# A fourteenth pair of tiles by seven half-size products, and the mLSTM steps of the fourth head set closer

## Chip, cores and metric

One core of one Trainium2 chip runs the whole program. The metric is the device time of one execution in microseconds; less is better. The time before is the median of three runs.

## What is computed

One layer of a hybrid encoder on 1088 columns (1024 of a prompt, 64 of a sample), all in float32: a combined input projection of the normalised x, an mLSTM branch of four heads, a convolution branch, the merge of both, and a feed-forward part. Cut to what matters here:

```python
xn = rmsnorm(x, p['norm_mix_pre'])
proj = xn @ p['w_in']                                  # q, k, v, o, i, f, u (2 x 1024), gates (2 x 1024)
h, C, n, m = mlstm(q, k, v, ig, lf, C, n, m)           # 4 heads, in chunks, a carry C from chunk to chunk
ya = (rmsnorm_heads(h) * jax.nn.sigmoid(o)) @ p['w_proj_a']
glu = u[..., :D_B] * jax.nn.sigmoid(u[..., D_B:])
c, conv_buf = causal_dwconv(glu, conv_buf, p['conv_dw'], p['conv_b'])
c = jax.nn.silu(layernorm(c, p['conv_ln_g'], p['conv_ln_b']))
yb = c @ p['w_proj_b'] + p['b_proj_b']
gt = jax.nn.sigmoid(gates + p['b_merge'])
mix = (gt[..., :D_MODEL] * ya + gt[..., D_MODEL:] * yb) @ p['w_out']
```

## The kernel before

Each float32 product is made of three passes in a rounded format: a weight tile is split into a high part (fhi) and a rest (flo), and so is x (rows 0 to 7 of rx and rows 8 to 15); high by high, high by rest, rest by high. A full output tile is 128 rows by 1088 columns.

The input projection makes its 65 output tiles in two ways. Plain: three slots to a tile (364, 364, 360 columns), each 24 matmuls (`product`, lines 1072 to 1084). By pairs (`pairs`, in `PAIRS_B`): two tiles that belong together (the halves of u, or the two gates of the merge, "g") form a 2 x 2 block matrix with the halves of the columns, and seven half-size products replace eight, each in two column pieces (304 and 240) of 12 matmuls (L1238 to L1240), 14 half products to a pair. The sums of x that this needs overwrite the second halves of the columns in part of rx; the original of them is put aside in DRAM (scr_b12) before the pairs and loaded back at their end. Before there are 13 pairs: six of u and seven of g; the last tile of g is plain.

The order of the stage is written out by hand in tables at the top of the file. `SLOTS` lists the plain slots; slots from S_B (18) on stand behind the pairs: the small "gate" tile (the mLSTM's i and f), then k, v, q of heads 0 to 3, then ga 7 and gb 7, then o 1 to o 7. I count these from the gate on as places 0 to 101, without the six small products `SUM_AFTER` that sum for the layer norm's mean (mu) and variance (var). Tied to places are:

- the 36 steps of the mLSTM (`STEP_AT`; four heads of nine). A step at place s issues its scores in the middle of the product of s (transposes L1146, products L1149), its values behind the product of s+1 (L1166 to L1169), its transposes `rows_out` behind that of s+3 (L1178), its store at s+4. ACT copies what the scores need and takes an exp (L1539 to L1543), DVE multiplies it into wt (L2212, semaphore a_set), DVE adds up hn and updates the carry cb (L2220 to L2251), POOL takes one power, ACT copies the transposed rows to zs (L1566). `rows_out` waits for a_set of all scores issued up to its own place, since both write into one PSUM bank.
- the taps of the depthwise convolution on DVE (`TAPS_AT` in the pairs, 13 a pair; `TAPS_SLOT` in the places, here over 64 of them, two to five a place), 51 operations to each of eight blocks (L2294 and around it).
- the layer norm's passes: `PASS1` (subtract the mean, square) from place 71, `PASS2` (normalise, tanh, multiply, split) at 88 to 99. In `PASS2` ACT does a tanh (L1783) and an Identity (L1786) of 1088 columns in the block's place and a copy (L1791) in the next.

ACT, DVE, SP and POOL walk the same list of slots, each in its own fixed order, and wait on semaphores. In a slot ACT first does the copies and the exp of the scores, then the evacuation (L1600, or L1613 with tanh), at the end of a tile from the ninth on a minus of the next weights (L1499), then zs, hn and its square, then the layer norm's work.

Weights come in a ring of three buffers fraw/flo/fhi (`weights(n)`, L671; from the ninth tile on by POOL). In the pairs the same memory, with four more slots, is a ring of ten for the half weights: slot `aslot(i, prod)` = (7i + POS[prod] + 6) mod 10. `ring_free(n)` gives the half product after which ring buffer n of the plain weights is free of the last pair's. SP's order in the last pair is:

```python
                    else:
                        sp.wait_ge(grp_done, ring_free(N_A))
                        weights(N_A)
                        sp.wait_ge(grp_done, b_at(i, 5, 1))
                        sp.dma_start(rx[:, 0:4, HALF:T].bitcast(F32), scr_b12[0]).then_inc(const_in, 16)
                        sp.dma_start(rx[:, KB:KB + 4, HALF:T].bitcast(F32), scr_b12[1]).then_inc(const_in, 16)
                        sp.wait_ge(grp_done, ring_free(N_A + 1))
                        weights(N_A + 1)
```

N_A is 5, the gate tile. TensorE runs the pairs and then waits for these loads (`pe.wait_ge(const_in, 96)`) and for the last pieces' evacuation before the gate's first product (L1284). The order of the 14 half products is (1,0) (1,1) (5,0) (5,1) (6,0) (6,1) (2,0) (7,0) (7,1) (2,1) (4,0) (4,1) (3,0) (3,1).

Of the kernel before, what the change touches and what calls it, by code (L numbers as in the profile page):

```python
# [12 lines left out]
KB = D // P  # L13
# [42 lines left out]
def in_tiles():  # L56

    def pair(k):
        return [("ua", k), ("ub", k)]

    def head(h, kinds):
        return [(kind, 2 * h + b) for kind in kinds for b in range(2)]

    def one(kind, a, b):
        return [(kind, m) for m in range(a, b)]

    return (pair(0) + pair(1) + one("o", 0, 1)
            + [("gate", 0)] + head(0, "kvq") + head(1, "kvq") + head(2, "kvq") + head(3, "kvq")
            + [("ga", 7), ("gb", 7)] + one("o", 1, KB))


IN_TILES = in_tiles()
# [6 lines left out]
N_A = 5  # L79
S_B = 3 * XN + 3 * (N_A - 3)  # L80
PAIRS_B = [("u", 2), ("g", 0), ("g", 1), ("u", 3), ("g", 2), ("u", 4), ("g", 3), ("u", 5), ("g", 4), ("u", 6), ("g", 5),
           ("u", 7), ("g", 6)]
NB = len(PAIRS_B)
OPS = 7 * NB
POS = {1: 0, 5: 1, 6: 2, 2: 3, 7: 4, 4: 5, 3: 6}
# [18 lines left out]
def done(s):  # L104

    return s + 1 + (14 * NB if s >= S_B else 0)
# [12 lines left out]
def hi_of(n):  # L119
# [1 line left out]
    return n + 1 + (OPS if n >= N_A else 0)  # L121


SUM_AFTER = {S_B + 66: ("mu", 0), S_B + 67: ("mu", 1), S_B + 70: ("mu", 2),
             S_B + 83: ("var", 0), S_B + 86: ("var", 1), S_B + 87: ("var", 2)}


def in_slots():

    slots = []  # L130
    for r, at in enumerate(WSLOTS):
        slots.append(at)
        if r in SUM_AFTER:
            name, c = SUM_AFTER[r]
            slots.append(((name, 0), c))
# [31 lines left out]
STEPS = [(h, j) for h in range(NH) for j in range(NSTEP)]  # L167
FULL = [s for s, (t, c) in enumerate(SLOTS) if t[0] not in ("mu", "var")]
NTH_FULL = {s: r for r, s in enumerate(FULL)}
STEP_AT = [S_B + 22 + 2 * i for i in range(len(STEPS))]  # L170
STEP_IN = {at: i for i, at in enumerate(STEP_AT)}
STEPS_END = FULL[STEP_AT[-1] + 3]

# [8 lines left out]
def rows_before(i):  # L182

    return sum(at + 3 < STEP_AT[i] for at in STEP_AT)


def scores_before(i):

    return sum(at <= STEP_AT[i] + 3 for at in STEP_AT)

# [4 lines left out]

TAPS_AT = [6] + [12 + 13 * i for i in range(NB)]
TAPS_SLOT = [TAPS_AT[NB]]
for r_ in range(64):
    left_ = NOP * KB - TAPS_SLOT[-1]
    TAPS_SLOT.append(TAPS_SLOT[-1] + (2 if r_ < 10 else 5 if r_ < 22 else left_ // (64 - r_)))  # L200
N_BY_DVE = 8
BY_POOL = [sum(1 for i in range(N_BY_DVE, N_IN) if i % 3 == s) for s in range(3)]
C_STORED = 32 * KB // 2
# [27 lines left out]
STORE_SLOT = {k: S_B + r + 1 for r in range(len(TAPS_SLOT) - 1) for k in convs_by(TAPS_SLOT[r], TAPS_SLOT[r + 1])}  # L231


PASS1 = {FULL[S_B + 71 + 3 * k // 2]: k for k in range(KB)}
PASS2 = {FULL[S_B + at]: k for k, at in enumerate((88, 89, 91, 92, 94, 96, 97, 99))}
C_HI = (0, 2, 4, 12, 14, 6, 8, 10)
TANH_OUT = [t for t in IN_TILES if t[0] in ("ga", "gb", "o")]

# [90 lines left out]
def build(nc, x, wts, wdn, par, gate_par, c_in, conv_halo, ffn_halo, y_out, c_out, m_out,  # L329
# [200 lines left out]
    with ExitStack() as ctx:  # L530
# [137 lines left out]
        def _(sp):  # L668
# [101 lines left out]
            for s, ((kind, k), c) in enumerate(SLOTS):  # L770
# [79 lines left out]
                if s == SLOT["mu", 0, 0]:  # L850
# [4 lines left out]
                    for j in range(2):  # L855
                        sp.dma_start(cs[j][:, :], scr_c[j]).then_inc(cs_in[j], 16)
                j = PASS1.get(s - 1)
                if j is not None:
                    sp.wait_ge(xc_set, j + 1)
                    sp.dma_start(scr_xc[j], cs[j % 2][:, :]).then_inc(c_sto[j % 2], 16)  # L860
                    if j + 2 < KB:
                        sp.wait_ge(csq_sq, j + 1)
                        sp.wait_ge(c_sto[j % 2], C_STORED + 16 * (j // 2 + 1))
                        sp.dma_start(cs[j % 2][:, :], scr_c[j + 2]).then_inc(cs_in[j % 2], 16)
                if s == min(PASS2) - 2:
                    for j in range(2):
                        sp.wait_ge(c_sto[j], C_STORED + 16 * KB // 2)
                for j in range(KB):
                    if s == (min(PASS2) - 2 if j < 2 else min(PASS2) + 2 if j < 5 else STEPS_END):
                        sp.wait_ge(grp_done, done(s - 1))  # L870
                        sp.dma_start(fz[:, C_HI[j] + 1, :], scr_xc[j]).then_inc(blk_in[j], 16)
                if s == FULL[STEP_AT[-1] + 4] + 1:
                    for j in range(2):
# [616 lines left out]
        def _(act):  # L1490
# [54 lines left out]
            def values(i):  # L1545
                h, j = STEPS[i]
                p = i % 2
                if j:
                    act.wait_ge(nq_full, i + 1)
                    if i >= 2:  # L1550
                        act.wait_ge(zt_set, i - 1)
                    act.activation(hn[p][:, :], bank(5, 0, VW), ACT.Copy, scale=gt[:, 16 * j + 4 + h:16 * j + 5 + h])\
                        .then_inc(t1_set, 1)
                act.wait_ge(hn_set, i + 1)
                if i >= 2:
                    act.wait_ge(z_full, i - 1)
                act.activation(zt[p][:, :], hn[p][:, 0:DH], ACT.Square, accum_out=sm[p][:, 3:4]).then_inc(ssq, 1)
# [148 lines left out]
            for s, ((kind, k), c) in enumerate(SLOTS):  # L1706
# [64 lines left out]
                if i is not None:  # L1771
                    values(i)
                j = PASS1.get(s)
                if j is not None:
# [3 lines left out]
                    act.activation(csqt[:, :], cs[j % 2][:, :], ACT.Square).then_inc(csq_sq, 1)  # L1778
                j = PASS2.get(s)
                if j is not None:  # L1780
# [6 lines left out]
                                   scale=halfs[:, at:at + 1]).then_inc(nth, 1)  # L1787
                j = PASS2.get(s - 1)
                if j is not None:
# [302 lines left out]
        def _(dve):  # L2092
# [338 lines left out]
            for s, ((kind, k), c) in enumerate(SLOTS):  # L2431
# [36 lines left out]
                for todo in taps_at(s):  # L2468
                    taps(*todo)
                    if todo[2] == NOP:  # L2470
                        add_sum(todo[0])
                j = PASS1.get(s)
                if j is not None:
# [4 lines left out]
                    if j:  # L2478
                        add_square(j - 1)
                if s - 1 == max(PASS1):  # L2480
                    add_square(KB - 1)
                j = PASS2.get(s - 2)
                if j is not None:
                    dve.wait_ge(c_hi, j + 1)
                    dve.tensor_tensor(rz[:, C_HI[j] + 1, :], fz[:, C_HI[j] + 1, :], rz[:, C_HI[j], :].bitcast(F32),
                                      ALU.subtract).then_inc(c_lo, 1)
                j = PASS2.get(s)
                if j is not None:
# [424 lines left out]
```

## Time and profile before

| what | us |
|---|---|
| median of three runs | 1926.76 (1926.02 to 1927.43) |
| the profiled execution | 1926.55 |
| its span, first to last instruction | 1924.6 |
| TensorE (PE) busy | 1904.2, 99% |
| VectorE (DVE) busy | 1297.1, 67% |
| ScalarE (ACT) busy | 834.7, 43% |
| GpSimd (POOL) busy | 69.6, 4% |
| mean of what the DMA moved | 125 GB/s |

The profile is of one execution; times in it are counted from its first instruction. "Busy" is the union of an engine's instructions; a matmul's record is longer than its distance to the next, because matmuls overlap, so costs on TensorE are read from the distance of starts or from windows. L-numbers are lines of the kernel. A wait is put down to the semaphore that came last.

### The profile page before, as it was taken

What the parts mean: (1) busy time and instruction counts of PE and PEld (TensorE: products, weight loads), DVE (VectorE), ACT (ScalarE), POOL (GpSimd) and SP (SyncE); (2) the same over time, 40 slices, a digit from 0 to 9 for tenths busy, and PEclk for the clock granted to TensorE, in tenths of its full rate; (3) what the DMA queues carried; (4) which work ended last, traced back from release to release, by engine and by line L of the source; (5) the groups of instructions that cost most, each with busy time, mean ns of one, the idle gap of its engine ahead of it and who ended that gap; (6) DMA issues with size and microseconds to landing.
All of it is one profiled execution on the core that took longest, in us unless ns stands there. A gap on an engine that the chain in (4) does not pass through costs nothing.

```text
span 1924.6 us, 32360 instructions
## 1 busy us (share of the span) xinstructions
PE 1904.2 (99%) x13095; PEld 1880.2 (98%) x13095; DVE 1297.1 (67%) x1991; ACT 834.7 (43%) x1534; POOL 69.6 (4%) x122
## 2 busy tenths in 40 slices
PE   9999999999999999999999999999999999999997
PEld 8999999999999999999999999999999999999997
DVE  7798889697777725364444468977777676646363
ACT  5454444422333334573122345654455444645342
POOL 0000000011111111110000000000000000000000
PEclk9999999999999999999999999999999999999999
DMA  3323232454343348668131323221222122556654
GB/s 133 125 84 128 96 108 86 160 121 101 86 117 89 94 115 232 183 185 335 61 137 44 129 73 107 90 80 68 83 75 80 68 90 97 194 191 217 206 173 154
DMA packets 108675, 240.24 MB, mean 125 GB/s; under 512 B 19052, under 2 KB 58732, under 8 KB 108528
## 3 DMA queue, kind: packets, MB, share of 16 engines
q1 hardware_dynamic: 99600, 205.66, 31.5%
q0 software_dynamic: 8928, 32.51, 7.6%
q8 instruction: 105, 1.72, 0.4%
q14 instruction: 42, 0.34, 0.1%
HBM read 182.20 MB, written 55.94 MB: 124 GB/s over the span
## 4 chain that ended last, share of the span: by engine, by line
PE 90%; DVE 5%; ACT 2%; issue 1%; DMA 1%; SPq 0%; POOL 0%; DVEq 0%; ACTq 0%; POOLq 0%
PE ps L1079 12%; PE ps L1080 12%; PE ps L1081 12%; PE ps L1438 7%; PE ps L1436 7%; PE ps L1437 7%; PE ps L1238 4%; PE ps L1239 4%; PE ps L1240 4%; PE ps L1454 4%; PE ps L1455 4%; PE ps L1456 4%; PE ps L1169 1%; PE ps L1166 1%; PE ps L1149 1%
## 5 line engine op out<-in xcount | busy, mean ns | idle before, releaser
L1079 PE MATMUL ps<-rx,fhi 128*128 128x364 f32 (+2 forms) x1120 | 375.1, 335 | 1.2 <-DMA flo<-wts 1.1
L1080 PE MATMUL ps<-rx,fhi 128*128 128x364 f32 (+2 forms) x1120 | 364.4, 325 | 0.0
L1081 PE MATMUL ps<-rx,flo 128*128 128x364 f32 (+2 forms) x1120 | 364.2, 325 | 0.0
L1079 PEld LDWEIGHTS ps<-rx,fhi 128*128 128x128 f32 x1120 | 210.7, 188 | 4.0 <-issue 1.6
L1080 PEld LDWEIGHTS ps<-rx,fhi 128*128 128x128 f32 x1120 | 210.7, 188 | 1.3
L1081 PEld LDWEIGHTS ps<-rx,flo 128*128 128x128 f32 x1120 | 210.5, 188 | 0.0
L1454 PE MATMUL ps<-ghi,dhi 128*128 128x384 f32 (+1 forms) x528 | 173.2, 328 | 3.0 <-DVE glo L2733 2.2
L1455 PE MATMUL ps<-glo,dhi 128*128 128x384 f32 (+1 forms) x528 | 172.3, 326 | 0.0
L1456 PE MATMUL ps<-ghi,dlo 128*128 128x384 f32 (+1 forms) x528 | 172.3, 326 | 0.0
L2726 DVE TENSOR_TENSOR dlo<-draw,dhi 128x1408 fp32r<-128x1408 f32 x48 | 77.7, 1625 | 119.0 <-ACT dhi L1985 119.0
L1238 PE MATMUL ps<-rx,ahi 128*128 128x240 f32 (+1 forms) x416 | 120.3, 289 | 0.6 <-DVE v L2390 0.5
L1985 ACT ACTIVATE dhi<-draw 128x1408 fp32r<-128x1408 f32 x48 | 66.1, 1381 | 125.4 <-DMA draw<-wdn 125.3
L1239 PE MATMUL ps<-rx,ahi 128*128 128x240 f32 (+1 forms) x416 | 120.0, 288 | 0.0
L1240 PE MATMUL ps<-rx,alo 128*128 128x240 f32 (+1 forms) x416 | 119.8, 288 | 0.0
L1600 ACT ACTIVATE qkv<-ps 128x364 f32<-128x364 f32 (+1 forms) x72 | 34.1, 474 | 172.8 <-PE ps L1081 172.8
L1454 PEld LDWEIGHTS ps<-ghi,dhi 128*128 128x128 f32 x528 | 99.1, 188 | 4.6 <-DVE glo L2733 2.9
L1455 PEld LDWEIGHTS ps<-glo,dhi 128*128 128x128 f32 x528 | 99.1, 188 | 0.3
L1456 PEld LDWEIGHTS ps<-ghi,dlo 128*128 128x128 f32 x528 | 99.1, 188 | 0.0
L1878 ACT ACTIVATE ub<-ps 128x304 f32<-128x304 f32 (+1 forms) x132 | 50.9, 402 | 103.3 <-PE ps L1438 97.8
L2294 DVE SCALAR_TENSOR_TENSOR f_e<-f_s,hsum,f_e 128x559 f32<-128x559 f32 x120 | 95.6, 796 | 0.0
L2294 DVE SCALAR_TENSOR_TENSOR f_a<-glub,pars,f_a 128x559 f32<-128x559 f32 x120 | 95.5, 796 | 0.0
L1438 PE MATMUL ps<-rz,ulo 128*128 128x304 f32 (+1 forms) x320 | 92.8, 290 | 0.0
(345 smaller groups left out, 5329.9 us busy)
## 6 DMA issues: line engine op xcount, KB each, us to landing
draw<-wdn SPq DMA_DIRECT2D x48, 704.0 KB, 4.2
uraw<-wts SPq DMA_DIRECT2D x44, 512.0 KB, 4.4
fhi<-wts POOLq DMA_DIRECT2D x31, 512.0 KB, 7.2
flo<-wts POOLq DMA_DIRECT2D x31, 512.0 KB, 6.3
fraw<-wts SPq DMA_DIRECT2D x27, 512.0 KB, 3.8
araw<-wts SPq DMA_DIRECT2D x52, 256.0 KB, 2.8
scr_g<-cva SPq DMA_DIRECT2D x22, 512.0 KB, 2.6
graw<-scr_g SPq DMA_DIRECT2D x43, 192.0 KB, 4.0
```

Source lines behind the costliest of these rows:

```text
L1079: pe.matmul(b, hi[:, w], src[:, his[k], cols], start=(k == 0), stop=False)
L1080: pe.matmul(b, hi[:, w], src[:, los[k], cols], start=False, stop=False)
L1081: mm = pe.matmul(b, lo[:, w], src[:, his[k], cols], start=False, stop=(k == KB - 1))
L1238: pe.matmul(b, ahi[s][:, c], bhi[:, k, :], start=(fresh and k == 0), stop=False, skip_group_check=True)
L1239: pe.matmul(b, ahi[s][:, c], blo[:, k, :], start=False, stop=False, skip_group_check=True)
L1240: mm = pe.matmul(b, alo[s][:, c], bhi[:, k, :], start=False, stop=(k == 3), skip_group_check=True)
L1436: pe.matmul(b, whi[:, c], bhi[:, k, :], start=(fresh and k == 0), stop=False, skip_group_check=True)
L1438: mm = pe.matmul(b, wlo[:, c], bhi[:, k, :], start=False, stop=(k == 3), skip_group_check=True)
L1454: pe.matmul(b, dhi[n % 2][:, kk], ghi[g % N_G][:, 0:w], start=(k == 0), stop=False, skip_group_check=True)
L1455: pe.matmul(b, dhi[n % 2][:, kk], glo[g % N_G][:, 0:w], start=False, stop=False, skip_group_check=True)
L1456: mm = pe.matmul(b, dlo[n % 2][:, kk], ghi[g % N_G][:, 0:w], start=False, stop=(k == FB - 1), skip_group_check=True)
L2294: dve.scalar_tensor_tensor(acc[:, :], src[:, i:i + w], tapw, acc[:, :], ALU.mult, ALU.add).then_inc(tap, 1)
```

## The change

The fourteenth pair ("g", 7) joins the list, and the plain tiles ga 7 and gb 7 leave it, with their six slots. Everything that depends on the number of pairs or slots follows by the tables: the rings' turns, the taps (13 more in the pairs), the counts of semaphores. The places are now 0 to 95. The fourth head's nine steps stand at 75, 76, 77, 79, 80, 81, 83, 84 and 86; heads 1 and 2 begin at 39 and 57 with a distance of two as before. mu and var move eight and six or seven places up, both passes of the layer norm seven and six. The taps left for the places are spread over 56 of them instead of 64.

```diff
@@ in_tiles
             + [("gate", 0)] + head(0, "kvq") + head(1, "kvq") + head(2, "kvq") + head(3, "kvq")
-            + [("ga", 7), ("gb", 7)] + one("o", 1, KB))
+            + one("o", 1, KB))
@@
 PAIRS_B = [("u", 2), ("g", 0), ("g", 1), ("u", 3), ("g", 2), ("u", 4), ("g", 3), ("u", 5), ("g", 4), ("u", 6), ("g", 5),
-           ("u", 7), ("g", 6)]
+           ("u", 7), ("g", 6), ("g", 7)]
@@
-SUM_AFTER = {S_B + 66: ("mu", 0), S_B + 67: ("mu", 1), S_B + 70: ("mu", 2),
-             S_B + 83: ("var", 0), S_B + 86: ("var", 1), S_B + 87: ("var", 2)}
+SUM_AFTER = {S_B + 58: ("mu", 0), S_B + 59: ("mu", 1), S_B + 62: ("mu", 2),
+             S_B + 77: ("var", 0), S_B + 79: ("var", 1), S_B + 80: ("var", 2)}
@@
-STEP_AT = [S_B + 22 + 2 * i for i in range(len(STEPS))]
+STEP_AT = [S_B + (22, 39, 57, 75)[h] + (2 * j if h < 3 else 11 * j // 8) for h, j in STEPS]
@@
-for r_ in range(64):
+for r_ in range(56):
     left_ = NOP * KB - TAPS_SLOT[-1]
-    TAPS_SLOT.append(TAPS_SLOT[-1] + (2 if r_ < 10 else 5 if r_ < 22 else left_ // (64 - r_)))
+    TAPS_SLOT.append(TAPS_SLOT[-1] + (2 if r_ < 10 else 5 if r_ < 22 else left_ // (56 - r_)))
@@
-PASS1 = {FULL[S_B + 71 + 3 * k // 2]: k for k in range(KB)}
-PASS2 = {FULL[S_B + at]: k for k, at in enumerate((88, 89, 91, 92, 94, 96, 97, 99))}
+PASS1 = {FULL[S_B + 64 + 3 * k // 2]: k for k in range(KB)}
+PASS2 = {FULL[S_B + at]: k for k, at in enumerate((82, 83, 85, 86, 88, 90, 91, 93))}
```

## Rows read from the trace of the kernel before

**Rows 1.** The page: busy time by engine, and the chain by engine.
```profile
PE 1904.2 (99%) x13095; PEld 1880.2 (98%) x13095; DVE 1297.1 (67%) x1991; ACT 834.7 (43%) x1534; POOL 69.6 (4%) x122
...
PE 90%; DVE 5%; ACT 2%; issue 1%; DMA 1%; SPq 0%; POOL 0%; DVEq 0%; ACTq 0%; POOLq 0%
```

**Rows 2.** Window: us, busy of PE, PEld, DVE, ACT, POOL; clock; DMA share, GB/s.
```profile
355.40:879.20 523.80, 522.74 (x3152) 509.43 (x3152) 346.55 (x706) 223.75 (x480) 67.02 (x104) 1.00 0.50 134
```

**Rows 3.** TensorE's waits, 355 to 880 us: total us, times, longest.
```profile
PE ps L1079 <- DMA flo<-wts: 1.1, 1, 1.1
```

**Rows 4.** Windows of one line's matmuls: ten pairs (L1240), twelve slots (L1081).
```profile
122.92:334.26 211.34, 161.50 (x560) 105.82 (x561) 1.00 0.31 106
...
367.37:415.28 47.91, 31.54 (x96) 18.03 (x96) 1.00 0.42 106
```

**Rows 5.** Timeline of SP's issues in the last pair: start us, us, what.
```profile
340.31 0.33 SPq L671 DMA_DIRECT2D fraw<-wts  x1
340.69 0.59 SPq L751 DMA_DIRECT2D rx<-scr_b  x1
...
349.35 0.35 SPq L671 DMA_DIRECT2D fraw<-wts  x1
```

**Rows 6.** Timeline of TensorE where the pairs end.
```profile
355.22 0.33 PE L1284 MATMUL ps<-rx,fhi 128*128 128x364 f32 x1
```

**Rows 7.** Windows of the last pair; DMA share and GB/s stand last.
```profile
341.50:343.20 1.70, 1.70 (x17) 1.70 (x16) 1.65 (x3) 0.42 (x1) 0.00 (x0) 1.00 0.79 269
343.20:349.60 6.40, 6.40 (x53) 6.40 (x53) 1.50 (x4) 2.12 (x4) 0.00 (x0) 1.00 0.91 346
349.60:350.60 1.00, 1.00 (x10) 1.00 (x9) 1.00 (x3) 0.00 (x0) 0.00 (x0) 1.00 0.38 111
```

**Rows 8.** DMA issues from 320 to 375 us: KB each, median us to landing.
```profile
fraw<-wts SPq DMA_DIRECT2D x3, 512.0 KB, 3.8
```

**Rows 9.** Timeline of DVE: two taps, then the step and its wait.
```profile
625.46 0.80 DVE L2294 SCALAR_TENSOR_TENSOR f_a<-glub,pars,f_a 128x559 f32<-128x559 f32 x1
626.17 0.80 DVE L2294 SCALAR_TENSOR_TENSOR f_d<-glub,pars,f_d 128x560 f32<-128x560 f32 x1
...
629.16 0.43 DVE L2220 TENSOR_TENSOR hn<-ps,hn 128x257 f32<-128x257 f32 x1 [1.48 <-ACT hn L1552]
```

**Rows 10.** The chain that ended last, two successive steps of the first head.
```profile
459.44 0.87 PE ps L1166 x4
470.70 0.87 PE ps L1166 x4
```

**Rows 11.** Timeline of TensorE: rows_out behind a slot, scores in the next.
```profile
796.85 0.38 PE L1178 MATMUL ps<-ident,zt 128*128 128x128 f32 x2
...
801.23 0.60 PE L1146 MATMUL ps<-ident,qkv 128*128 128x128 f32 x4
```

**Rows 12.** Timeline of ACT in the fourth head, beside the layer norm's second pass.
```profile
822.63 0.45 ACT L1613 ACTIVATE spl<-ps 128x360 f32<-128x360 f32 x1
822.98 1.05 ACT L1499 ACTIVATE flo<-fhi 128x1024 fp32r<-128x1024 f32 x1
823.93 0.61 ACT L1566 ACTIVATE zs<-ps,mnq 128x128 f32<-128x128 f32 x2
824.43 0.48 ACT L1552 ACTIVATE hn<-ps,gt 128x257 f32<-128x257 f32 x1
...
825.82 1.28 ACT L1783 ACTIVATE fz<-fz,halfs 128x1088 f32<-128x1088 f32 x1
827.13 1.30 ACT L1786 ACTIVATE fz<-fz,halfs 128x1088 f32<-128x1088 f32 x1
828.34 1.10 ACT L1791 ACTIVATE rz<-fz 128x1088 fp32r<-128x1088 f32 x1
829.34 0.36 ACT L1539 ACTIVATE vt<-ps 128x256 f32<-128x256 f32 x1
```

**Rows 13.** Timeline of DVE: the product of the scores that follow these.
```profile
830.29 0.29 DVE L2212 TENSOR_TENSOR wt<-ps,wt 128x128 f32<-128x128 f32 x1 [2.52 <-ACT wt L1543]
```

## The prediction

> **What bounds the kernel now.** I read the page first: TensorE is busy 1904.2 of 1924.6 us and holds 90% of the chain that ended last [rows 1]. So a change pays only by taking matmuls away or by a wait of TensorE that it ends, and costs what it makes TensorE wait. Next the windows by stage: from the first gate product at 355.4 us to the end of the input projection at 879.2 TensorE is busy 522.7 of 523.8 us at a granted clock of 1.00 [rows 2], and the list of waits has a single one in that stretch, 1.1 us for the last weight tile [rows 3]. There is no idle time to win in the stage that the change reorders. The question is what the new order makes late.
>
> **The matmuls, removed and added.** The two last gate tiles leave the list of slots, six slots of 24 matmuls; a fourteenth pair of 14 half products of 12 matmuls comes in. Ten pairs (560 matmuls of one line, 56 a pair) took 211.34 us, 21.13 each; twelve plain slots without a step (96 of one line, 8 a slot) took 47.91 us, 3.99 each [rows 4]. Removed 6 x 3.99 = 23.95 us, added 21.13: TensorE gets 2.8 us back. The 36 mLSTM steps, the six sums for mu and var and everything behind the stage are the same work. The evacuations (tanh of six slots against ACT and DVE pieces, sums and splits of the half weights) lie beside TensorE in both forms: thirteen pairs run at the matmuls' own pace already, so the fourteenth costs its matmuls.
>
> **The restored half of x: a queue that is moved.** During the pairs half of the columns of rx holds sums; the original was put aside in scr_b12 and SP loads it back (2 x 1088 KB) during the last pair, because the gate tile behind the pairs needs it (PE's wait for const_in 96). SP does that behind `wait ring_free(N_A)`, then weights(5), then the two loads. ring_free(5) is the last use of ring slots 0 and 1 of the ten slots for half weights. They turn with the number of pairs, slot = (7i + POS + 6) mod 10. For i = 12 slots 0 and 1 are products 1 and 5, the first four of the last pair's 14. For i = 13 they are products 2 and 7: the wait moves to the tenth of 14. In the trace of before SP issued weights(5) at 340.31 and the reloads from 340.69, and weights(6), whose wait was for the same tenth product, at 349.35 [rows 5]. The gate's first matmul followed the pairs at 355.22, without a gap [rows 6]. So SP will issue the reload with only 6.0 us of products left, instead of 15.
>
> How long it takes: behind the issue of the weights the DMA moved 269 GB/s to 343.2 (the weights), 346 GB/s to 349.6 (6.4 us x 346 = 2.2 MB, the reload) and fell to 111 GB/s in the last microsecond [rows 7]. From 340.31 that is 9.3 us to the fall, 10.3 to the end of that window. After the change both transfers stand in the same queue in the same order. From 349.35 the reload lands at 358.7 to 359.7 of the old clock, and TensorE, ready at 355.4, **waits 3.3 to 4.3 us; I take 3.8**. Before, the same landing lay 4.8 us ahead of its use, which is why no row shows a wait. Bounds: 2.75 MB at the 346 GB/s of the best window with nothing around it are 7.9 us, 6.0 of them covered, so 1.9 us; and 4.5, if the last packets and their signal take as long as they can in these windows. Behind the waiting gate matmuls stands all of TensorE; nothing catches up, because it is the bound.
>
> Other things hang on the same wait. ACT takes weights(5) in its order ahead of the last two product-4 pieces: it lands some 3.8 us after its issue [rows 8], at 353.1, its copy of 1024 columns takes about 1 us, the pieces reach to 355: just in time, nothing more than the reload. weights(6) now waits for the last product, lands behind the reload at about 361, and is wanted when the gate's 8 us are over (367): covered by the gate tile; if the reload were early, its slack would still be 2 us. weights(7) follows it. All other moves of SP, the neighbours' nb, c_out and cb transfers, have two or more slots of slack; 0.
>
> **The taps.** With 13 more taps in the pairs, 227 are left for 56 slots; the last eleven get five each, where before no slot with steps had more than four. In a two-slot period with eight taps DVE waits 1.48 us for ACT's hn, and a tap follows the last at 0.71 us [rows 9]: two more take 1.42. It fits by a hair; a lag recovers and TensorE's use of DVE's results is a slot later. 0, up to 1.
>
> **The steps closer together.** A step with two slots takes 11.25 us (459.44 to 470.70 [rows 10]); less 2 x 3.99 that is 3.27 on TensorE. 2.38 of it are rows_out and values (796.85 to 801.23 less half a product of 2.0 [rows 11]), 0.87 the scores. Heads 1 and 2 start one place earlier and keep the spacing of two: 0. The fourth head stands at 75, 76, 77, 79, 80, 81, 83, 84, 86. Before, scores and rows_out never fell in one slot. Now they do at 79, 80, 83, 84, 86, and rows_out waits for a_set of the scores begun half a product, 2.0 us, earlier, since both use one bank. Normally a_set is there 1.1 us ahead of it. At 79 and 80 nothing else is large on ACT: 0. From 82 on the layer norm's second pass is there too. I follow ACT from the end of place 82's product (0): TensorE does rows_out and values to 2.4, place 83 ends at 7.3, its rows_out at 7.5, scores of 84 at 9.5 to 10.3, product end 12.3, where rows_out wants a_set. ACT from 7.3, by the distance of successive starts [rows 12]: evacuation 0.35, minus 0.95, two zs 0.5 (823.93 to 824.43), then tanh 1.3, Identity 1.2 and the copy of the block before 1.0: 12.6. Only then the new scores' vt, kw and exp up to DVE's product, 0.95 (829.34 to 830.29), and the product itself, 0.3 [rows 12, 13]: 13.9. TensorE **waits 1.6 us** at place 84. Place 83 has 0.5 us left by the same count, place 86 0.5. Bounds: 0 (ACT half a block ahead) and 3 (83 and 86 lose theirs too). Layer norm's first pass keeps its pattern, seven places earlier; the six sums move with it; from place 87 on (eight before the last) everything stands as before, the 1.1 us for the last weights included.
>
> **Sum.** -2.8 + 3.8 + 1.6 = +2.6 us. The profiled execution took 1926.55 us (span 1924.6 and 1.95 around it), 0.2 under the median of the three runs, 1926.76. So 1926.55 + 2.6 = 1929.2, 1929.3 against the median. A measurement of this kernel can tell 0.2%, 3.9 us, from no change: this is +0.13%, within it.
>
> **The clock at the gap.** The granted clock is 1.00 across every stretch read and the longest wait in the stage is 1.1 us [rows 2, 3]; a gap of 3.8 us has no like in the trace. The Trainium skill (TensorE: Matmul & The Clock Gate, Part 1) says that an idle stretch takes the array to 1.2 GHz, and activity back to 2.4: this speaks against the change, and no row here shows it. By rows, the gate tile is 8 us of matmuls at 2.4 GHz (355.4 to 363.4); at 1.2 it would take up to 8 more, at least 0. By that rule the sum would be between +2.6 and +10.6.
>
> **The rivals.**
> - *The reload hides after all and the steps don't bite:* the time is 1926.8 - 2.8 = 1924.0. For it: nothing waited there before. Against: the transfer's 7.9 us are more than the 6.0 left. 6 in 100. To be over 0.2% faster something unseen must go too, as the last weights' 1.1 us.
> - *The clock falls at the gap (slower):* place, the gate tile; price 0 to 8 us, middle 4; it decides from a drop that lasts 1.3 us of TensorE's work. 1929.3 + 4 = 1933.3. For: the gap is near three times any wait of the stage. Against: it is short, and the matmuls around it are dense. 12 in 100.
> - *ACT becomes the bound in the fourth head (slower):* its backlog of 5.3 us a slot against a slot of 4.86 repeats at 83, 84 and 86 with evacuations late as well: 3 waits of 1.6 to 2 in place of one, +3.5: 1932.8. For: ACT is the only engine near full there. Against: places 84 and 85 bring no new block beyond one. 14 in 100.
> - *The reload stalls and the steps are free:* 1927.7, inside the forecast's range.
>
> **The numbers.** Forecast 0.62 (with the last rival in it; own range 1925.9 to 1931.5: -2.8 + 1.9 + 0 to -2.8 + 4.5 + 3), hidden 0.06, clock 0.12, ACT 0.14, others 0.06. The range reaches from the hidden case's 1924.0 to 1933.5, which leaves out the clock's upper half and tails. Slower by over 0.2% (above 1930.6): the two slower rivals, 0.24, and a sixth of the forecast's range; 0.34 rounded to 0.32 for their mild halves. Faster 0.05, same 0.63.
>
> **What would show it.** Right: in SP's order the loads of rx come after 349.35 + 21.1 = 370.5; TensorE's list of waits has a new row at the gate's line, L1284, of 3.3 to 4.3 us put down to the DMA rx<-scr_b or const_in; a wait of 1 to 3 us at rows_out's line L1178 on DVE's wt in the fourth head, and no other new row over 1 us; the stage from the gate to the end of the projection is 22.4 us shorter (23.95 less 1.6). Wrong: no gate wait (the loads were faster), a granted clock under 1 behind it, waits of TensorE on ACT's evacuations, or DVE late for mu.

## The result, and the profile after

The changed kernel takes **1930.1 us**, the median of nine runs (1929.19 to 1933.14); the kernel before, on the same chip, 1926.38 (1924.92 to 1927.43). The recorded ratio is 1.0023, 95% interval 1.0014 to 1.0032. The change is slower: by 3.7 us between the medians, just inside the 0.2% (3.9 us) that the prediction called no change, and by 0.23% (4.4 us) by the ratio, just outside it. The interval lies on both sides of that mark. Forecast were 1929.3 and +2.6. The profiled execution took 1929.81 us.

The page of the changed kernel: its span, busy time by engine, and TensorE's busy tenths.

```profile
span 1928.0 us, 32466 instructions
PE 1902.0 (99%) x13119; PEld 1878.2 (97%) x13119; DVE 1305.4 (68%) x2008; ACT 839.3 (44%) x1543; POOL 66.9 (3%) x118
...
PE   9999999899999999999999999999999999999997
```

TensorE is busy 2.2 us less than in [rows 1], and the span is 3.4 us longer. The one 8 among TensorE's tenths is the slice from 337 to 386 us: the gap is there. Next the waits of TensorE in the changed kernel from 370 to 885 us, the stretch in which [rows 3] had one row:

```profile
PE ps L1284 <- DMA rx<-scr_b: 5.3, 1, 5.3
PE ps L1178 <- issue: 1.5, 1, 1.5
PE ps L1079 <- DMA flo<-wts: 1.0, 1, 1.0
```

Both new rows are at the lines that the prediction named. The second was foretold at 1.6. The first is 5.3 where 3.8 was foretold. Here is TensorE's own timeline where the pairs end (start, duration, what, idle before it); [rows 6] answers to it:

```profile
375.43 0.28 PE L1240 MATMUL ps<-rx,alo 128*128 128x240 f32 x1
380.96 0.67 PE L1284 MATMUL ps<-rx,fhi 128*128 128x364 f32 x1 [5.26 <-DMA rx<-scr_b]
381.43 0.51 PE L1285 MATMUL ps<-rx,fhi 128*128 128x364 f32 x1
...
384.43 0.33 PE L1285 MATMUL ps<-rx,fhi 128*128 128x364 f32 x1
...
390.58 0.32 PE L1079 MATMUL ps<-rx,fhi 128*128 128x364 f32 x1
```

Behind the gap a matmul takes 0.51 us, and from 384.43 on 0.33. The windows of the same stretch name the reason; the granted clock stands ahead of the DMA's share and its GB/s:

```profile
375.80:381.00 5.20, 0.04 (x1) 0.04 (x1) 0.34 (x1) 1.59 (x2) 2.10 (x6) 1.00 1.02 391
381.00:382.40 1.40, 1.40 (x5) 1.40 (x6) 0.00 (x0) 0.00 (x0) 0.00 (x0) 0.50 0.98 398
382.40:384.00 1.60, 1.60 (x7) 1.60 (x6) 0.48 (x1) 1.06 (x1) 0.00 (x0) 0.50 0.46 188
...
385.44:388.10 2.66, 2.66 (x18) 2.66 (x18) 2.66 (x5) 2.06 (x4) 0.00 (x0) 1.00 0.00 0
```

From 381.0 to 384.0 the engine had 1.2 of its 2.4 GHz, after 5.3 us without a matmul; it got the rest back while it worked. From the last matmul of the pairs to the first of the tile behind the gate (L1079) it is 390.58 - 375.43 = 15.15 us. In the kernel before the same two matmuls stand at

```profile
355.10 0.28 PE L1240 MATMUL ps<-rx,alo 128*128 128x240 f32 x1
...
363.19 0.33 PE L1079 MATMUL ps<-rx,fhi 128*128 128x364 f32 x1
```

8.09 us apart. The loss is 7.06 us. TensorE starts the gate tile 5.4 us later behind the pairs, which is the wait, and the tile takes 9.62 us (380.96 to 390.58) where it took 7.97 (355.22 to 363.19): 1.65 us of half clock. I call this distance **D**; it serves in all experiments below.

The issues of SP in the changed kernel, to be held against [rows 5]:

```profile
369.71 0.33 SPq L671 DMA_DIRECT2D fraw<-wts  x1
370.09 0.59 SPq L751 DMA_DIRECT2D rx<-scr_b  x1
370.72 0.63 SPq L752 DMA_DIRECT2D rx<-scr_b  x1
375.73 0.83 SPq L671 DMA_DIRECT2D fraw<-wts  x2
```

The reload is issued with 5.6 us of products left. And the place in the fourth head: ACT's timeline in the changed kernel, from the evacuation at the end of place 83's product to that of place 84, and TensorE's first instruction behind its wait ([rows 12] show the same operations before):

```profile
823.72 0.47 ACT L1613 ACTIVATE spl<-ps 128x360 f32<-128x360 f32 x1 [0.91 <-PE ps L1081]
824.09 1.05 ACT L1499 ACTIVATE flo<-fhi 128x1024 fp32r<-128x1024 f32 x1
825.04 0.62 ACT L1566 ACTIVATE zs<-ps,mnq 128x128 f32<-128x128 f32 x2
825.53 1.30 ACT L1783 ACTIVATE fz<-fz,halfs 128x1088 f32<-128x1088 f32 x1
826.87 1.30 ACT L1786 ACTIVATE fz<-fz,halfs 128x1088 f32<-128x1088 f32 x1
828.07 1.09 ACT L1791 ACTIVATE rz<-fz 128x1088 fp32r<-128x1088 f32 x1
829.07 0.36 ACT L1539 ACTIVATE vt<-ps 128x256 f32<-128x256 f32 x1
...
829.69 0.30 ACT L1543 ACTIVATE wt<-wt 128x128 f32<-128x128 f32 x1
```

```profile
830.03 0.29 DVE L2212 TENSOR_TENSOR wt<-ps,wt 128x128 f32<-128x128 f32 x1 [4.23 <-ACT wt L1543]
```

```profile
830.42 0.41 PE L1178 MATMUL ps<-ident,zt 128*128 128x128 f32 x2 [1.54 <-issue]
```

The three long operations of the layer norm's second pass stand between the evacuation and the scores' copies, in the order in which the prediction laid them out; from 823.72 to vt at 829.07 it is 5.35 us, and the prediction counted 5.3 (7.3 to 12.6). The profile puts TensorE's wait down to "issue", that is, to nothing that it shows. The kernel has rows_out wait for DVE's product of the scores (L2212), and that product, held up for ACT's exp until 830.03, ends at 830.3, 0.1 us before TensorE starts.

**The sum.** The window from the end of the pairs to the end of the input projection, in the changed kernel ([rows 2] is the same stretch before):

```profile
375.72:884.12 508.40, 500.60 (x3009) 487.07 (x3010) 338.00 (x694) 219.81 (x473) 64.35 (x100) 1.00 0.50 136
```

It is 15.4 us shorter (523.8 before): 23.95 less 7.06 and 1.5 is 15.4. With the 21.13 us of the fourteenth pair that makes +5.7. The spans differ by 3.4, so 2.3 lie outside the stage. The first matmul of the pairs starts at 78.28 us, before at 79.08; in the other runs below this start falls anywhere from 77.95 (e10) to 79.72 (e1), whatever the kernel, so these 0.8 are scatter. The rest, 1.5, lies behind the stage, where TensorE's waits show 1.1 of it: at L1454 2.2 us for glo and 0.8 for dlo before, 1.5 and 0.6 after, at L1436 0.8 before and 0.6 after. From the first matmul behind the projection (879.05 before, 883.94 after) to the end of the span it is 1045.6 us before, 1045.2 and 1045.1 in the two other kernels with 13 pairs (e2, e5), 1044.1 in the changed kernel and 1044.2 to 1045.0 in the eight others with 14 pairs. By the means of the two kinds some 0.9 us of the 1.5 come with the new order in every such kernel, and the rest is scatter. Why the waits are shorter is open.

### The profile page after: what moved, and what is told of

Its sections match the earlier page's. It is cut to its first block, busy times and chain, and to the rows that moved or that the text cites. A ratio compares the mean times of both kernels' runs of the same rounds, so it can differ in the third digit from the quotient of the medians.

```text
span 1928.0 us, 32466 instructions
## 1 busy us (share of the span) xinstructions
PE 1902.0 (99%) x13119; PEld 1878.2 (97%) x13119; DVE 1305.4 (68%) x2008; ACT 839.3 (44%) x1543; POOL 66.9 (3%) x118
## 4 chain that ended last, share of the span: by engine, by line
PE 92%; DVE 4%; DMA 2%; ACT 1%; issue 1%; SPq 0%; POOL 0%; DVEq 0%; ACTq 0%; POOLq 0%
PE ps L1079 12%; PE ps L1081 12%; PE ps L1080 12%; PE ps L1438 7%; PE ps L1436 7%; PE ps L1437 7%; PE ps L1238 5%; PE ps L1239 5%; PE ps L1240 5%; PE ps L1454 4%; PE ps L1455 4%; PE ps L1456 4%; PE ps L1169 2%; PE ps L1166 1%; PE ps L1149 1%
## 5 line engine op out<-in xcount | busy, mean ns | idle before, releaser
L1079 PE MATMUL ps<-rx,fhi 128*128 128x364 f32 (+2 forms) x1072 | 359.4, 335 | 1.1 <-DMA flo<-wts 1.0
L1080 PE MATMUL ps<-rx,fhi 128*128 128x364 f32 (+2 forms) x1072 | 348.6, 325 | 0.0
L1081 PE MATMUL ps<-rx,flo 128*128 128x364 f32 (+2 forms) x1072 | 348.5, 325 | 0.0
L1079 PEld LDWEIGHTS ps<-rx,fhi 128*128 128x128 f32 x1072 | 201.7, 188 | 3.7 <-issue 1.5
L1080 PEld LDWEIGHTS ps<-rx,fhi 128*128 128x128 f32 x1072 | 201.7, 188 | 1.3
L1081 PEld LDWEIGHTS ps<-rx,flo 128*128 128x128 f32 x1072 | 201.5, 188 | 0.0
L1454 PE MATMUL ps<-ghi,dhi 128*128 128x384 f32 (+1 forms) x528 | 173.2, 328 | 2.1 <-DVE glo L2733 1.5
L1238 PE MATMUL ps<-rx,ahi 128*128 128x304 f32 x448 | 129.6, 289 | 0.6 <-DVE v L2390 0.5
L1239 PE MATMUL ps<-rx,ahi 128*128 128x304 f32 x448 | 129.2, 288 | 0.0
L1240 PE MATMUL ps<-rx,alo 128*128 128x304 f32 x448 | 129.0, 288 | 0.0
L1454 PEld LDWEIGHTS ps<-ghi,dhi 128*128 128x128 f32 x528 | 99.1, 188 | 3.6 <-DVE glo L2733 2.2
```

What stands on the lines that cost most here:

```text
L1079: pe.matmul(b, hi[:, w], src[:, his[k], cols], start=(k == 0), stop=False)
L1080: pe.matmul(b, hi[:, w], src[:, los[k], cols], start=False, stop=False)
L1081: mm = pe.matmul(b, lo[:, w], src[:, his[k], cols], start=False, stop=(k == KB - 1))
L1238: pe.matmul(b, ahi[s][:, c], bhi[:, k, :], start=(fresh and k == 0), stop=False, skip_group_check=True)
L1239: pe.matmul(b, ahi[s][:, c], blo[:, k, :], start=False, stop=False, skip_group_check=True)
L1240: mm = pe.matmul(b, alo[s][:, c], bhi[:, k, :], start=False, stop=(k == 3), skip_group_check=True)
```

## The experiments

All ten (e1 to e10) were timed in five rounds beside the kernel before, whose median was 1926.24 us beside e1 to e4, 1925.84 beside e5 to e8, 1926.25 beside e9 and 1926.35 beside e10. The theory at the start: the change is worth -2.8 us of matmuls, the reload behind the late wait costs 7 (a wait and the half clock behind it), and the steps 1.5. The rivals: the loss at the gate is the clock's and not the load's; the load is slow because other transfers share its way; the steps cost nothing or much more.

**e1. The reload first.** On the changed kernel, SP issues the reload ahead of the wait for the ring, and the gate's weights behind it:

```diff
-                        sp.wait_ge(grp_done, ring_free(N_A))
-                        weights(N_A)
                         sp.wait_ge(grp_done, b_at(i, 5, 1))
                         sp.dma_start(rx[:, 0:4, HALF:T].bitcast(F32), scr_b12[0]).then_inc(const_in, 16)
                         sp.dma_start(rx[:, KB:KB + 4, HALF:T].bitcast(F32), scr_b12[1]).then_inc(const_in, 16)
+                        sp.wait_ge(grp_done, ring_free(N_A))
+                        weights(N_A)
```

> The changed kernel with SP's order in the last pair turned: the two reloads of rx right behind product (5,1), weights(5) behind them with its own wait. Theory (the loss is the late reload): the wait of 5.3 us at L1284 is gone, and with it the 3.4 us at half clock that followed it (1.7 us), so 7.0 us less than the changed kernel: about 1923.1, and 3 us under the kernel before; the 1.5 us at L1178 stays. Rival (the gate tile is late for another reason, its weights or the pieces of product 4, which weights(5) still delays): a wait of 2 us or more stays at L1284 and the gain over the changed kernel is under 4 us.

Measured: 1924.44 us (1924.16 to 1926.23, 11 runs), ratio to before 0.9992 (0.9983 to 1.0001), 5.7 us under the changed kernel. Of its waits of TensorE from 350 to 885 us the one at the gate, and ACT at the gate's evacuation:

```profile
...
PE ps L1284 <- ACT g L1594: 1.4, 1, 1.4
...
```

```profile
380.78 1.06 ACT L1494 ACTIVATE fhi<-fraw 128x1024 fp32r<-128x1024 f32 x1 [2.03 <-DMA fraw<-wts]
...
383.38 0.47 ACT L1594 ACTIVATE g<-ps 4x364 f32<-4x364 f32 x1
```

The wait for rx is gone and the half clock with it; D is 386.67 - 376.86 = 9.81. A new wait took 1.4 of the gain: ACT stands for 2.0 us in the copy of the next weights, which its order puts ahead of the gate's evacuation, and TensorE's third gate product, for a bank of PSUM, waits until ACT has emptied it (L1594, done at 383.85; TensorE goes on at 383.89). In the changed kernel the late reload had hidden that. So the late reload is the cause of the loss at the gate, and the next wait in the queue was 1.4 us long.

**e2. The late reload alone, in the kernel before.** Nothing of the change but the moment of the wait: the tenth product of the last of 13 pairs.

```diff
-                        sp.wait_ge(grp_done, ring_free(N_A))
+                        sp.wait_ge(grp_done, b_at(i, 2, 1))
```

> The kernel before (13 pairs), with weights(5) and the reload held back until the tenth half product of the last pair, as the ring makes it in the changed one. Theory: a wait of 4 to 5.5 us on the DMA rx<-scr_b at L1284 appears here too, without any fourteenth pair, perhaps with some us at half clock behind it: 4 to 7 us slower than before, about 1930.4 to 1933.4. Rival (the wait belongs to the fourteenth pair's own traffic): under 2 us slower.

Measured: 1932.36 us (1930.57 to 1934.56, 5 runs), ratio 1.0035 (1.0022 to 1.0047), +6.1. The window of the gap with the first matmuls behind it, and TensorE's first matmul after it:

```profile
356.40:363.20 6.80, 3.81 (x13) 3.81 (x14) 1.41 (x2) 1.06 (x1) 0.13 (x2) 0.50 0.98 363
```

```profile
359.39 0.67 PE L1284 MATMUL ps<-rx,fhi 128*128 128x364 f32 x1 [5.09 <-DMA rx<-scr_b]
```

A wait of 5.1 us, half clock behind it for 3.8 us, D = 369.15 - 354.02 = 15.13: the changed kernel's loss at the gate, from one moved wait, without a fourteenth pair and without closer steps.

**e3 and e6. The gap filled with matmuls.** To part the clock from the wait: small matmuls of a constant into a bank not in use stand ahead of TensorE's wait for rx, first 46, then 23.

```diff
                     pairs()
+                    pe.wait_ge(c11_set, 2 * NB)
+                    for _ in range(46):
+                        pe.matmul(bank(7, 0, P), ones[:, :], ident[:, :], start=True, stop=True)
                     pe.wait_ge(const_in, 96)
```

> The changed kernel with 46 small matmuls (ones by ident into an idle PSUM bank, result unused, some 4.9 us) between the last half product and the wait for the reload; nothing is left out. Theory (the idle engine loses its clock, and the first gate matmuls pay 1.7 us): the granted clock stays at 1.00 through the gate tile, its first product takes 2.7 us instead of 4.5, and the time is 1.7 us under the changed kernel's, about 1928.4; the reload lands when it did. Rival (the clock falls for another reason, or its fall costs nothing): no difference, 1930.1 within 0.5.

Measured: 1933.76 us (1933.35 to 1935.32, 5 runs), ratio 1.0042 (1.0029 to 1.0054). The groups of TensorE from 375 to 387 us:

```profile
L1249 PE MATMUL ps<-ident,ones 128*128 128x128 f32 x92 | 10.4, 275 | 0.0
```

46 instructions stand there as 92, from 375.29 to the gate's first matmul at 385.48: 10.2 us, where I had counted on about 5. The filling was twice too long and ended 4.5 us behind the moment at which TensorE began in the changed kernel (380.96). The clock stayed at 1.00 in every window, as expected, but the time says nothing. So again with half as many:

> The test of the busy gap again, with 23 small matmuls instead of 46: each of them runs as two passes of 0.107 us, so 46 filled 9.8 us and ended 4.9 us behind the landing; 23 fill 4.9 of the 5.3. Theory: the clock stays at 1.00, the first gate product ends 1.7 us earlier than in the changed kernel, time 1928.4. Rival (the fall of the clock costs nothing): 1930.1 within 0.5.

Measured: 1930.34 us (1928.35 to 1931.06, 11 runs), ratio 1.0021 (1.0012 to 1.003). Two windows, in the filling and behind it, and two of the waits:

```profile
376.00:381.50 5.50, 5.50 (x52) 5.50 (x51) 1.06 (x3) 2.44 (x3) 2.14 (x6) 1.00 1.05 362
383.00:385.00 2.00, 2.00 (x14) 2.00 (x13) 0.00 (x0) 0.58 (x1) 0.00 (x0) 1.00 0.53 217
```

```profile
PE ps L1079 <- DMA flo<-wts: 1.4, 1, 1.4
PE ps L1287 <- DMA rx<-scr_b: 0.6, 1, 0.6
```

No half clock, and D = 390.77 - 376.66 = 14.11, 1.04 less than in the changed kernel although the gate tile began 6.03 us behind the last matmul of the pairs (382.69), where it was 5.53. The tile itself took 8.08 us in place of 9.62. But TensorE then waited 0.4 us longer for the last weights, and the medians do not differ (1930.34 and 1930.1). What the profiles show is that the half clock follows the idle time and that without it the gate tile is 1.5 us shorter; what it is worth in the whole time I could not resolve. It is the smaller part in any case: the load is the cause.

**e4. The next weights held back.** Does the reload take long because weights(6) and (7), issued at 375.73, share its way? On the changed kernel:

```diff
                         sp.wait_ge(grp_done, ring_free(N_A + 1))
+                        sp.wait_ge(const_in, 96)
                         weights(N_A + 1)
```

> The changed kernel with SP holding weights(6) and weights(7) back until the reload has landed. Theory (these two, issued at 375.7 while the reload was under way, share the DMA engines with its last third and made the wait 5.3 instead of the 3.8 forecast): the wait at L1284 falls to 3.8 to 4.6 us, and k 0's first product then waits for its weights only if they take over 7 us. Time 1 us under the changed kernel, or less if the half clock falls otherwise. Rival (the reload is slow by itself): the wait stays at 5.0 to 5.5 us.

Measured: 1930.28 us (1929.4 to 1931.44, 11 runs), ratio 1.0023 (1.0014 to 1.0032), no gain. The wait at the gate is 4.7 instead of 5.3. Whether these 0.6 are the price of sharing is not settled. From the issue of weights(5) to TensorE's start it is 11.25 us in the changed kernel and 10.69 here, but 11.75 in e6 (370.94 to 382.69), which makes the same transfers as the changed kernel: one profile each, and a scatter of 0.5. The windows of the reload (issued from 370.17 on) and the first gate matmul:

```profile
369.80:378.30 8.50, 5.99 (x48) 5.79 (x46) 1.88 (x4) 3.94 (x5) 2.14 (x6) 1.00 0.88 309
...
378.80:380.50 1.70, 0.01 (x1) 0.01 (x1) 0.00 (x0) 0.00 (x0) 0.00 (x0) 1.00 0.10 37
```

```profile
380.49 0.43 PE L1285 MATMUL ps<-rx,fhi 128*128 128x364 f32 x1 [4.71 <-DMA rx<-scr_b]
```

The DMA's rate in 40 equal steps of 0.35 us from 368 to 382 us:

```profile
GB/s 0 0 0 0 0 0 0 70 140 187 246 339 406 301 323 342 336 361 385 404 392 395 348 373 367 385 404 410 429 317 87 50 50 50 12 0 0 0 94 70
```

This is the larger part of the overshoot. With nothing beside it the transfer is all but over at 378.8, and TensorE starts 1.7 us later. In that time the queues move 37 GB/s, at a tenth of the sixteen engines' time: a few last packets until about 380.2 (10.4 us behind the issue of the weights), and TensorE goes on at 380.49. The fall of the rate is not the landing.

The shorter wait brought nothing: D is 390.62 - 375.51 = 15.11, as in the changed kernel. The half clock came here too, from 381.07 on, 0.6 us after TensorE had begun again, and the third product of the gate waited 0.2 for ACT, whose copy of the held-back weights was now late.

**e5. The closer steps alone, in the kernel before.** The fourth head at 81, 82, 83, 85, 86, 87, 89, 90 and 92 (six behind the changed kernel's), with 13 pairs and the layer norm where it was.

```diff
-STEP_AT = [S_B + 22 + 2 * i for i in range(len(STEPS))]
+STEP_AT = [S_B + (22 + 2 * i if h < 3 else 81 + 11 * j // 8) for i, (h, j) in enumerate(STEPS)]
```

> The kernel before (13 pairs, 102 places) with the fourth head alone set at 81, 82, 83, 85, 86, 87, 89, 90, 92, where the changed kernel has it relative to the layer norm's second pass. Theory (scores and rows_out in one slot wait for ACT's backlog): one wait of 1.5 us at L1178, near place 90, and 1 to 2 us slower than before, about 1927.7; no wait at L1284 and no half clock. Rival (closer steps cost nothing, the wait at L1178 belongs to the shortened stage): the time of before within 0.5.

Measured: 1932.22 us (1931.7 to 1933.11, 5 runs), ratio 1.0032 (1.0019 to 1.0045), +6.4. Waits of TensorE, ACT ahead of the longest, and the window behind it:

```profile
PE ps L1146 <- ACT kw L1540: 4.4, 2, 3.0
PE ps L1178 <- issue: 1.5, 2, 0.9
```

```profile
770.63 1.11 ACT L1778 ACTIVATE csqt<-cs 128x1088 f32<-128x1088 f32 x1 [4.77 <-DVE csq L2327]
771.64 0.37 ACT L1539 ACTIVATE vt<-ps 128x256 f32<-128x256 f32 x1
```

```profile
773.00:776.00 3.00, 3.00 (x21) 3.00 (x22) 0.17 (x1) 0.00 (x0) 0.00 (x0) 1.00 1.00 366
```

L1178 costs the 1.5 that it costs in the changed kernel, in two parts. The other 4.4 are of a kind that I had not thought of: in this arrangement the last blocks of the first pass fall among the closer steps, ACT waits 4.8 us in its order for DVE's square (L2327), and the scores' copies wait behind it. The clock stayed at 1.00 behind this gap of 3.0 us. That the change's earlier layer norm avoids these late copies is how I read it, for e5 also keeps the taps and the six sums where they were, and no run moved the first pass alone. This run shows the 1.5 at L1178 again; it does not price the steps alone.

**e7. The evacuation of the gate freed.** On e1: ACT's copy of weights(6) moves from the end of the pairs to behind the gate's first evacuation, DVE's rest of it likewise.

```diff
@@ ACT, end of the pairs
-                whole(N_A + 1)
@@ ACT, each slot
                 evac(s, kind, k, c)
+                if s == S_B:
+                    whole(N_A + 1)
@@ DVE, end of the pairs
-                rest(N_A + 1)
@@ DVE, each slot, behind the taps
+                if s == S_B:
+                    rest(N_A + 1)
```

> The kernel with the reload first, and ACT's copy and DVE's rest of the k 0 weights (weights(6), which now land 4 us behind the pairs) moved from ahead of the gate's first evacuation to behind it. Theory (the 1.4 us at L1284 on ACT's g come from ACT sitting in that copy's wait while the gate's first piece is ready): that wait goes, 1.4 us under the reload-first kernel, about 1923.0. Rival (the copy is then late for k 0): a wait on flo of as much at L1079.

Measured: **1923.38 us** (1922.44 to 1924.45, 11 runs), ratio 0.9986 (0.9978 to 0.9995).

```profile
PE ps L1178 <- issue: 1.5, 1, 1.5
PE ps L1079 <- DMA flo<-wts: 0.7, 1, 0.7
```

D is 384.66 - 376.40 = 8.26, within 0.2 of the kernel before. Both losses at the gate are gone, and what the fourteenth pair promises by its matmuls is there: from the first matmul of the pairs to the last of the projection it is 798.4 us (79.27 to 877.66), 799.8 before (79.08 to 878.88), 1.4 less for the -2.8 of matmuls and 1.5 of the steps. The whole time fits only with the part behind the stage that I cannot explain: 1925.84 (before, in this series) - 2.8 + 1.5 - 1.5 is 1923.0.

**e8. The second pass later.** On e7, to take the backlog out of ACT's way at place 84, the second block of the second pass goes from 83 to 84.

```diff
-PASS2 = {FULL[S_B + at]: k for k, at in enumerate((82, 83, 85, 86, 88, 90, 91, 93))}
+PASS2 = {FULL[S_B + at]: k for k, at in enumerate((82, 84, 85, 86, 88, 90, 91, 93))}
```

> The same with the layer norm's second block in place 84 instead of 83, so that ACT comes to the scores of place 84 without that block's tanh and Identity (2.5 us) ahead of them. Theory: the wait of 1.5 us at L1178 goes; at most 0.5 comes back at place 86, where the copy of that block now stands ahead of the scores: 1.0 to 1.5 us less again, about 1921.8. Rival (the backlog only moves): a wait of 1 us or more at place 86, or at the last weights, and no gain.

Measured: 1924.52 us (1923.71 to 1926.07, 11 runs), ratio 0.9994 (0.9985 to 1.0003), 1.1 us more than e7. TensorE's timeline at place 86, and the window behind it:

```profile
837.83 0.66 PE L1178 MATMUL ps<-ident,zt 128*128 128x128 f32 x2 [2.36 <-issue]
```

```profile
837.80:841.00 3.20, 3.17 (x11) 3.20 (x12) 3.20 (x3) 2.26 (x4) 1.46 (x2) 0.50 0.67 223
```

The rival was right: the wait moved two places on and grew, and now it, too, is followed by half clock.

**e9 and e10. The steps themselves further apart.** On e7, the fourth head's eighth block goes from place 84 to 85, then (e10, with 12 in place of the 11 below) its ninth from 86 to 87 as well.

```diff
-STEP_AT = [S_B + (22, 39, 57, 75)[h] + (2 * j if h < 3 else 11 * j // 8) for h, j in STEPS]
+STEP_AT = [S_B + (22, 39, 57, 75)[h] + (2 * j if h < 3 else (0, 1, 2, 4, 5, 6, 8, 10, 11)[j]) for h, j in STEPS]
```

> e7 (the gate's reload issued first, and the evacuation of the gate's half taken out of the engines' way) with the fourth head's block (3,7) at place 85 instead of 84; (3,8) stays at 86 and the four later ones at 87, 89, 91 and 92 stay as in e7. Place 84 then has no scores, and what ACT must finish before rows_out there has one block's pieces fewer. Theory (the wait at L1178 is ACT's queue at place 84 and nothing else): the 1.5 us wait is gone, at most 0.5 us of it comes back at place 86; span about 1.3 us under e7's 1922.0, ratio to before about 0.9978. Rival (the backlog only moves, as with the second pass one place later): a wait of 1 us or more at L1178 at place 85 or 86, no gain over e7's 1923.4, perhaps with a half clock behind it as in e8.

> As e9_step_at_85, and the fourth head's last block (3,8) at place 87 instead of 86. e9 had its 1.6 us at L1178 at place 86: ACT waited 2.08 us for DVE (L2495), so the second pass's tanh and Identity of place 85 came at 831.45 to 834.0, ahead of the scores' copies of place 86, and rows_out of the same place waits for those scores. Now no place from 84 on has scores and rows_out together (scores at 85 and 87, rows_out at 84, 86, 88 and 90). Theory (a wait at L1178 needs scores and rows_out in one place behind a piece of the second pass): the list of TensorE's waits from 370 to 885 us has no row at L1178 over 0.3 us, the granted clock stays 1.00, span about 1920.3 and 1921.8 us in the runs, ratio 0.9977. Rival (ACT's backlog reaches the scores themselves or the values): a new wait of 1 us or more at L1166 or L1146 in place of it, span again 1921.8 and 1923 us in the runs.

Measured: 1923.12 us (1922.33 to 1925.53, 11 runs), ratio 0.9984 (0.9975 to 0.9993), and 1922.84 us (1922.5 to 1923.88, 11 runs), ratio 0.9983 (0.9974 to 0.9992). First the wait of e9, at place 86, and what ACT did ahead of it; then the wait list of e10, its only row from 370 to 885 us, and the longer of the two waits in it on the timeline:

```profile
835.33 0.41 PE L1178 MATMUL ps<-ident,zt 128*128 128x128 f32 x2 [1.63 <-issue]
```

```profile
831.45 1.30 ACT L1784 ACTIVATE fz<-fz,halfs 128x1088 f32<-128x1088 f32 x1 [2.08 <-DVE fz L2495]
...
833.98 0.36 ACT L1539 ACTIVATE vt<-ps 128x256 f32<-128x256 f32 x1
```

```profile
PE ps L1079 <- ACT spl L1613: 2.3, 2, 1.7
...
863.49 0.43 PE L1079 MATMUL ps<-rx,fhi 128*128 128x364 f32 x1 [1.72 <-ACT spl L1613]
```

In e9 the wait moved to place 86, as its rival said. In e10 the theory's condition was met and L1178 waits nowhere, but an evacuation that ACT reaches late takes its place. TensorE's waits in the stretch come to 2.2 us in e7 and 2.3 in e9 and e10, and the medians of the three (1923.38, 1923.12, 1922.84) are too close to be told apart. So place 84's wait is not an accident of one place. Ahead of the late tanh in e9 ACT itself had waited 2.1 us for DVE (L2495), and 5.8 us at the same line ahead of the late evacuation in e10. That DVE sets the pace of the second pass is a reading of such rows; no run tried it with less work on DVE.

## Why the prediction was right, and which terms were mis-sized

**What bounds the kernel** (right). TensorE fills 99% before and after, and every microsecond of the result is a matmul taken away or a wait that it got.

**The matmuls, -2.8** (right). 21.13 and 23.95 close the sum of the stage to a tenth. e7, with the gate's loss taken away, has the pairs and the stage 1.4 us shorter together, which is -2.8 and the 1.5 of the steps; its 2.5 us in the medians hold the open part behind the stage as well.

**The restored half of x, 3.8** (mechanism right, size wrong; the wait 5.3). The issue came at 370.1, where 370.5 was said, behind the wait for the tenth product, and e2 shows that this wait alone makes the loss. The failing step is how the landing was read: "9.3 us to the fall, 10.3 to the end of that window", from the rate of all queues, with the middle taken. TensorE could start only 10.7 us after the issue of the weights (e4, nothing beside it), since the last packets trickle on until 10.4 us; that is the upper end and 0.4 more. The trickle could not be read off the kernel before, because weights(6), issued at 349.35, was in the way there: the DMA moved 70 GB/s from 349.6 to 350.1 and 207 after it, so the 111 GB/s of the last window in [rows 7] are not the load's alone. In the changed kernel it was 11.25 us. Of weights(6) the prediction said that it "lands behind the reload at about 361"; it, and weights(7) with it, went beside the reload instead, when about half of the bytes were still to come (239 GB/s from 369.71 to 375.73 are 1.4 of the 2.75 MB). What that cost is not settled: 0.6 between the profiles of e4 and the changed kernel, with a scatter of 0.5. The upper bound of 4.5 was under both waits, 4.7 and 5.3.

**weights(6), "covered by the gate tile"** (held in the changed kernel, and only because the reload was as late). "If the reload were early, its slack would still be 2 us" was wrong: with the reload early TensorE waited 1.4 us, since ACT stood in the copy of these weights ahead of the gate's evacuation (e1). The count had looked at who needs the weights, not at what is queued behind their copy.

**The clock** (counted as a rival with 12 in 100; it happened, and was small). The granted clock fell to 0.50 for about 3 us and cost 1.7, where the rival had 0 to 8 and 4 in the middle. The Trainium skill (TensorE: Matmul & The Clock Gate, Part 1) has idle time take the array to 1.2 GHz and activity bring it back to 2.4; the trace agrees, with 5.3 us of idle ahead of the fall and 1.7 lost. In the profiled execution the clock's mean over the span is 0.997; in six of the nine executions it was 0.996, and these took 1931.2 us in the mean against 1929.7 of the other three, so elsewhere the fall may have cost more. The chance was set too low: a gap of 3 to 4 us was forecast, and the argument "it is short" rested on no row. Certain it was not either, as the gap of 3.0 us in e5 shows, which had full clock behind it. The threshold named for it, a drop worth 1.3 us of work, was passed, yet the medians stayed inside the 3.9 us, because of the 1.5 us at the end, which the forecast did not have, and the 0.8 at the start, which are scatter. The sign "22.4 us shorter" for the stage from the gate on came out as 20.8 (503.16 from 380.96 to 884.12, against 523.98 from 355.22 to 879.20); the half clock is the difference.

**The taps, heads 1 and 2, 0** (right). No wait of TensorE stands there.

**The steps closer together, 1.6** (right: 1.5, at the place and with ACT's order as told). Places 83 and 86 had no wait, as counted. What the text took as moved at no cost, the layer norm's first pass "seven places earlier", may well be the condition for that number (e5, which has the steps closer without it, waits 4.4 us more; but e5 differs in the taps and the sums too). The rival's "3 waits of 1.6 to 2 in place of one" did not come.

**The sum.** -2.8 + 3.8 + 1.6 = +2.6 was said; it was -2.8 + 7.06 + 1.5 = +5.7 in the stage and +3.4 in the span. Of the gate's 3.3 too little, 1.5 were the landing and 1.7 the clock; 2.3 were given back outside the stage, unforeseen, and for the most part not explained. The forecast of 1929.3 was right to 0.8 us partly because errors of both signs met.

## What to carry to other kernels

When a count changes that ring slots turn with, look at every wait that is written by slot number: here one more pair moved a wait from the fourth to the tenth of 14 products and took 9 us of lead (14.5 before, 5.5 after) from a load that stands behind it in the queue, and issuing the load ahead of that wait gave 5.7 us back. Count a load as landed when the last packets' trickle is over, not when the rate falls. Count a gap of TensorE of 5 us with its half clock behind it (1.7 us here), and one of 2 to 3 us as a case that may or may not have it. And expect the next wait in line: of the 7 us at the gate 1.4 came back on ACT until its order was mended too, and in the fourth head three ways to remove a 1.5 us wait only moved it.

## What the runs showed of the hardware that I had not expected

- Half clock behind a wait of only 2.4 us: 0.50 from 837.8 to 841.0 us in e8. Yet the gap of 3.0 us in e5 had full clock behind it, as had those of 1.5 to 1.7 in the changed kernel, e9 and e10. The length of a gap by itself does not tell whether the clock falls. In e4 the clock fell only at 381.07, 0.6 us after TensorE had begun again (380.49); its matmuls went from 0.33 to 0.51 us while it worked.
- A float32 matmul of a 128 x 128 constant by 128 columns stands in the trace as two, each 0.11 us after the last (92 for 46, 10.2 us), where I had counted on one of about 0.11.
- A 2.2 MB load that runs at over 300 GB/s ends with 1.7 us at 37 GB/s (e4) before the waiting engine goes on.
